# A decoder trunk on one core: the cross-attention's cached keys, cached values and memory projections in another order

## The reference

```python
def cross_attend(h, mk, mv, w_q, w_o):
    B, T, D = h.shape
    q = (h @ w_q).reshape(B, T, XATTN_HEADS, XATTN_HEAD_DIM)
    s = jnp.einsum('bthd,bmhd->bhtm', q, mk).astype(F32) * (XATTN_HEAD_DIM ** -0.5)
    p = jax.nn.softmax(s, axis=-1).astype(mv.dtype)
    o = jnp.einsum('bhtm,bmhd->bthd', p, mv).reshape(B, T, D)
    return o @ w_o
```

## Time and profile before

| | |
|---|---|
| median of 3 runs | 1862.55 us (1862.42 to 1863.79) |
| the profiled execution | 1862.46 us, span 1860.7 us |
| mean granted TensorE clock | 0.924 of full |
| busy: TensorE, DVE, ACT, GpSimd | 88%, 54%, 38%, 17% |
| cross-attention, from the norm's reciprocal to the output projection's start | 557.7 to 676.1 us (layer 0), 1476.3 to 1594.6 us (layer 1) |

### The profile page before, as it was taken

One profiled execution on the slowest core, in us unless ns is written; L12 is line 12 of the kernel. 1 busy time (PEld: TensorE's weight loads), 2 busy tenths in 40 slices (PEclk: granted clock), 3 DMA queues, 4 the chain that ended last, 5 costly groups with the idle time before them and its releaser, 6 DMA issues.

```text
span 1860.7 us, 32204 instructions
## 1 busy us (share of the span) xinstructions
PE 1645.3 (88%) x13842; PEld 1546.5 (83%) x13842; DVE 1008.2 (54%) x1467; ACT 711.2 (38%) x1206; POOL 319.2 (17%) x365
## 2 busy tenths in 40 slices
PE   7999989884779988999989998999755999799997
PEld 6999979772578868999989998988634997699996
DVE  5554467854455336554365544786564533465543
ACT  4443345221344324443344433452123443344432
POOL 0000006994010000000000001089920100100000
PEclk9999999886789989999989999998767999799999
DMA  5766634101534774445345575330034357634450
GB/s 223 264 246 256 245 117 139 39 2 37 182 145 141 298 285 136 159 165 175 136 158 204 207 297 202 136 114 20 2 115 159 114 212 281 254 136 159 161 175 30
DMA packets 39246, 303.66 MB, mean 163 GB/s; under 512 B 4736, under 2 KB 4896, under 8 KB 6304
## 3 DMA queue, kind: packets, MB, share of 16 engines
q1 hardware_dynamic: 36624, 287.67, 42.6%
q0 software_dynamic: 2192, 12.35, 2.2%
q10 hardware_dynamic: 288, 1.57, 0.2%
HBM read 291.82 MB, written 36.83 MB: 177 GB/s over the span
## 4 chain that ended last, share of the span: by engine, by line
PE 66%; POOL 15%; DVE 9%; ACT 4%; DMA 3%; issue 1%; SPq 0%; POOLq 0%; DVEq 0%; ACTq 0%
PE bank L565 21%; PE bank L566 20%; PE bank L567 20%; POOL arena L462 10%; POOL arena L478 4%; DMA slots<-stream 3%; ACT w_hi L1202 2%; DVE w_lo L1590 1%; DVE h_mem L1605 1%; DVE h_lo L1590 1%; DVE rs L1600 1%; PE bank L576 1%; PE bank L1118 1%; PE bank L1154 1%; PE bank L1103 1%
## 5 line engine op out<-in xcount | busy, mean ns | idle before, releaser
L1590 DVE TENSOR_TENSOR w_lo<-slots,w_hi 128x1024 fp32r<-128x1024 f32 x392 | 481.6, 1231 | 452.8 <-ACT w_hi L1202 452.3
L565 PE MATMUL bank<-h_hi,w_hi 128*128 128x288 f32 x2048 | 619.1, 302 | 39.3 <-DVE h_lo L1590 30.5
L566 PE MATMUL bank<-h_lo,w_hi 128*128 128x288 f32 x2048 | 611.2, 298 | 0.0
L567 PE MATMUL bank<-h_hi,w_lo 128*128 128x288 f32 x2048 | 609.1, 297 | 0.0
L1202 ACT CAST w_hi<-slots 128x1024 fp32r<-128x1024 f32 x392 | 410.1, 1048 | 392.0 <-PE bank L567 344.9
L565 PEld LDWEIGHTS bank<-h_hi,w_hi 128*128 128x128 f32 x2048 | 389.7, 190 | 48.3 <-DVE h_lo L1590 36.5
L567 PEld LDWEIGHTS bank<-h_hi,w_lo 128*128 128x128 f32 x2048 | 392.5, 192 | 0.0
L566 PEld LDWEIGHTS bank<-h_lo,w_hi 128*128 128x128 f32 x2048 | 391.8, 191 | 0.2
L566 PE MATMUL bank<-hid_lo,w_hi 128*128 128x288 f32 x704 | 208.2, 296 | 0.0
L565 PE MATMUL bank<-hid_hi,w_hi 128*128 128x288 f32 x704 | 208.1, 296 | 0.0
L567 PE MATMUL bank<-hid_hi,w_lo 128*128 128x288 f32 x704 | 206.8, 294 | 0.0
(11 more groups left out here) (281 smaller groups left out, 1939.7 us busy)
## 6 DMA issues: line engine op xcount, KB each, us to landing
slots<-stream SPq DMA_DIRECT2D x244, 1024.0 KB, 5.0
out_win3k<-win3k SPq DMA_DIRECT2D x2, 4080.0 KB
out_win3v<-win3v SPq DMA_DIRECT2D x2, 4080.0 KB
out_win2k<-win2k SPq DMA_DIRECT2D x2, 2032.0 KB
out_win2v<-win2v SPq DMA_DIRECT2D x2, 2032.0 KB
con<-consts SPq DMA_DIRECT2D x1, 2276.0 KB, 11.9
arena<-mem_in POOLq DMA_DIRECT2D x2, 1024.0 KB, 5.5
out_memk<-arena POOLq DMA_DIRECT2D x2, 1024.0 KB, 7.4
```

The source lines that it names most:

```text
L565: mm(out, lhs[0], rhs[0], start=start, stop=False)
L566: mm(out, lhs[0], rhs[1], start=False, stop=False)
L567: return mm(out, lhs[1], rhs[0], start=False, stop=stop)
L1590: D(tt(out, src, hi.bitcast(F32), ALU.subtract), name)
```

## The change

The slab order from kv 2 on becomes: kv 2, memk 0, kv 3, memk 1, memk 2, memk 3, kv 4, memk 4, memk 5, kv 5, memk 6, memk 7, kv 6, memv 0, memv 1, kv 7, memv 2 to 7, then o 0 to 3 as before (slabs 63 to 88). TensorE's order follows: after the prompt's scores come the samples' scores in pairs with the value blocks between them, then the samples' transposed probabilities and products with cached values two by two around value block 3, and the last four among the prompt's heads. On ACT the samples' exponentials and the copies of their transposed probabilities move ahead of value block 3's copies. On DVE row maxima come earlier, and the samples' `row_max(4)` and `weigh(4)` move in among the splits.

```diff
-for _i in range(MEMK_EARLY):
-    ORDER.remove(("memk", _i))
-    ORDER.insert(ORDER.index(("kv", _i + K_EARLY // 2)) + 1, ("memk", _i))
+_x = ORDER.index(("kv", K_EARLY // 2))
+_after_q = (("kv", (2,)), ("memk", (0,)), ("kv", (3,)), ("memk", (1, 2, 3)), ("kv", (4,)), ("memk", (4, 5)), ("kv", (5,)),
+            ("memk", (6, 7)), ("kv", (6,)), ("memv", (0, 1)), ("kv", (7,)), ("memv", range(2, 8)))
+ORDER[_x:ORDER.index(("o", 0))] = [(_name, _i) for _name, _some in _after_q for _i in _some]
```

TensorE, where `memory_values(n)` is the value block as before and `sample_values(b_)` one step of the former loop over the samples (for b_ = 0 with the wait for the samples' transposed probabilities in front):

```diff
+                memory_keys((4, 5))
+                sample_scores(0)
+                memory_keys((6, 7))
+                sample_scores(1)
+                prompt_scores()
+                sample_scores(2)
+                sample_scores(3)
+                memory_values(0)
+                sample_scores(4)
+                sample_scores(5)
+                memory_values(1)
+                sample_scores(6)
+                sample_scores(7)
+                memory_values(2)
+                probs_T(8)
+                sample_values(0)
+                sample_values(1)
+                memory_values(3)
+                sample_values(2)
+                sample_values(3)
+                for hd in range(4):
+                    probs_T(2 * hd)
+                    probs_T(2 * hd + 1)
+                    if hd:
+                        prompt_out(hd - 1)
+                    sample_values(4 + hd)
+                prompt_out(3)
```

ACT, where `memory_values(n)` copies the block's two banks and then splits `next_unit(kv_unit(KT + 2 * n + 1))`:

```diff
+                for n in range(4):
+                    xexp(2 * n)
+                    split(next_unit(kv_unit(KT + 2 * n)))
+                    xexp(2 * n + 1)
+                    if n == 2:
+                        xexp(6)
+                        xexp(7)
+                        xexp(8)
+                        memory_values(2)
+                        sample_probs_T()
+                        split(next_unit(kv_unit(KT + 6)))
+                        memory_values(3)
+                        break
+                    memory_values(n)
```

DVE:

```diff
                 for u in range(8):
-                    if u % 2 == 0 and u < 6:
-                        row_max(u // 2 + 1)
+                    if u < 3:
+                        row_max(u + 1)
+                    if u == 4:
+                        row_max(4)
                     split(next_unit(kv_unit(KT + u)))
+                    if u == 4:
+                        weigh(4)
                     if u % 2:
                         weigh(u // 2)
-                row_max(4)
-                weigh(4)
```

More of the change, by code:

```diff
@@ L49 @@
 NSLOT = 4
-MEMK_EARLY = 6
 K_EARLY = 4
@@ L1107, in sample_scores, with prompt_scores, memory_values @@
                         TL.done(i, ("xs", 8))
[L1109 to L1121, removed]
+                def prompt_scores():
+                    pe.wait_ge(scalar_done, SL.value(l, ("kx", KT - 1)))
+                    for u in range(8):
+                        hd, qt = divmod(u, 2)
+                        if qt == 0:
+                            claim(hd, (SL, ("xexp", u + 1)))
+                        for dt in range(2):
+                            i = mm(bank[hd][:, qt * MEM:(qt + 1) * MEM], qx[:, 2 * hd + dt, qt * P:(qt + 1) * P], kx[:, 2 * hd + dt, :],
+                                   start=dt == 0, stop=dt == 1)
+                        TL.done(i, ("xs", u))
+                def memory_values(n):
                     for mt in range(2):
@@ L1135, in _ @@
                                 TL.done(i, ("vx", n * 2 + mt))
-                    sample_scores(n + 2)
-                for b_ in range(MEMK_EARLY, DEC_BATCH):
-                    sample_scores(b_)
                 def probs_T(u):
@@ L1156, in prompt_out, with sample_values @@
                     TL.done(i, ("ox", hd))
[L1158 to L1168, removed]
+                def sample_values(b_):
+                    if b_ == 0:
+                        claim(5, (SL, "oxs"))
+                        pe.wait_ge(scalar_done, SL.value(l, ("xpT", 8)))
                     w = arrived(SLAB_AT["memv", b_]).rearrange("p (k c) -> p k c", k=2)
@@ L1175, in _ @@
                     TL.done(i, ("slab", SLAB_AT["memv", b_]))
-                TL.done(i, "oxs")
+                    if b_ == DEC_BATCH - 1:
+                        TL.done(i, "oxs")
+                memory_keys((4, 5))
[25 more added lines that the diff above has]
+                prompt_out(3)
                 claim(4, (VL, "oxs_lo"))
@@ L1520, in _ @@
                     split(next_unit(kv_unit(KT + 2 * n + 1)))
-                xexp(8)
                 def probs_T(u):
@@ L1544, in _ @@
                         prompt_out(hd - 1)
-                sample_probs_T()
                 prompt_out(3)
```

## The result

The changed kernel takes 1895.81 us (median of 4 runs, 1891.49 to 1896.62) against 1862.49 us: a ratio of 1.0176, 95% interval 1.0157 to 1.0195, so it is slower by 1.8%. The prediction had 1880.5 us and a range up to 1891. Its profiled execution took 1891.49 us with a span of 1889.7 us.

The account below looks back on a forecast made before the run. TensorE, 88% busy, was taken as the bound, except at cross-attention's end, where it waits for value slabs. Three new waits with clock loss gave +10.8 and +9.4 us by layer, less 2.2: +18.0, 1880.5 us, range 1865 to 1891.

Parts of the forecast that it names:

- The ring: Cross-attention transfers: four slots, SyncE issues slab n only when slab n-4 is released, so kv 4, 5 and 7 come later.
- Rival A: Cross-attention: kv slabs arrive in time and TensorE runs through, 13.0 us per layer saved, 1836.5 us; chance 0.08.
- First wait: Before the prompt's scores: TensorE idles for key copies behind kv 4's split, 4.7 us in layer 0, 3.3 in layer 1.
- The clock behind each wait: After each TensorE wait over 2.2 us: work at half clock loses 1.8 us, bounds 0 and 2.3.
- What comes back: At the output projection's start: the 2.3 us lost at half clock partly disappears, 1.1 us per layer taken.
- Landings: Slab transfers: one lands about 5.0 us after issue, each of several issued closely 2.46 us after the one before.
- Second and third wait: Before value block 1, 4.5 us behind kv 5's split; before the samples' transposes, 6.1 us behind kv 7's.
- The tail: End of cross-attention: four heads of 2.16 us with four slabs of 0.93, 12.3 us, then copies and projection start.
- The value slabs: Cached value transfers: six of eight no longer issued after the whole of the scores; the last ones not late.
- B: Cross-attention: waits come but the clock stays up or its loss falls into the next wait, 1869.7 us; chance 0.08.
- C: Cross-attention: gain and waits cancel, time within 0.2% of no change, which needs the third wait to vanish; chance 0.04.
- D: Cross-attention: stores and paired issues delay further landings, 2 us on each of two more per layer, 1889 us; chance 0.05.

Follow-up runs that it names:

- a1: Changed kernel with only the slab order altered, kv 4 to 7 each one pair earlier: 1848.92 us, ratio 0.9921 to the first kernel.
- d1: Changed kernel plus 7, 10 and 13 products of constants on TensorE in its three waits: 1879.46 us, ratio 1.0081 to the first kernel.
- b4: Changed kernel with a1's slab order and the samples' softmax, transposes and first two cached values behind value block 3: 1858.27 us, ratio 0.9961.
- a0: The changed kernel run again, unchanged, with a second profile: 1894.04 us, ratio 1.0164 to the first kernel.

## Why the prediction was wrong in size

**The ring, right.** "Kv 4 takes the second of the pair issued at 602.5 and 602.9": it was issued at 602.2 as the second of a pair and landed after 8.1 us. The three waits came at the three places, with the releasers named (ACT, ACT, DVE), and a1 removes them by list order alone. Rival A's mechanism exists, but only in a1's order: its condition, kv 4 split before about 606.5, is met there (the split starts at 602.23).

**First wait, right.** 4.7 and 3.3 us predicted, 4.24 and 3.16 measured in the first profile.

**The clock behind each wait, mis-sized: the largest of four terms that failed.** "I take 1.8 for each wait over 2.2 us", 10.8 for six. The runs show 14 to 15.5: d1 gives 15.5 at most, 14 if its shorter waits are taken off. The windows behind the six waits of the changed kernel, layer 0 and then layer 1, give the same:

```profile
613.00:619.00 6.00, 6.00 (x16) 4.79 (x17) 0.77 (x1) 0.00 (x0) 0.57 (x1) 0.55 0.43 176
638.00:643.00 5.00, 4.80 (x25) 4.83 (x26) 4.53 (x9) 1.61 (x4) 0.00 (x0) 0.58 0.54 180
661.00:667.00 6.00, 5.38 (x43) 2.99 (x44) 1.36 (x3) 0.43 (x2) 0.00 (x0) 0.57 0.30 81
1547.00:1554.00 7.00, 6.61 (x17) 5.31 (x18) 1.32 (x2) 0.34 (x2) 0.57 (x1) 0.53 0.57 235
1572.00:1578.00 6.00, 6.00 (x30) 6.00 (x31) 4.11 (x9) 2.04 (x4) 0.00 (x0) 0.54 0.72 261
1594.00:1598.00 4.00, 2.96 (x26) 1.61 (x30) 1.80 (x5) 0.43 (x2) 0.00 (x0) 0.50 0.00 0
```

Length times (1 - clock), less half of the idle time inside the window, is 2.7, 2.0, 2.3, 3.1, 2.8 and 1.5 us: 14.4 in all, 2.4 for a wait where 1.8 was taken. The 1.8 came from the earlier trace rows, where the low stretch lasted 3.4 us. The bound of 2.3 was the other row at hand, the projection's, and three of the six reach or pass it. Two rows gave no upper bound.

**What comes back, wrong.** I took 1.1 us per layer for the projection at full clock. In the changed kernel its start again ran at half for 5.5 us in layer 0 and 3.4 in layer 1 (0.72 from 1624 to 1630), against 4.6 and 4.4 before. In sum nothing came back: 2.2 us.

```profile
691.00:697.00 6.00, 5.64 (x24) 5.67 (x25) 2.48 (x3) 0.78 (x1) 0.00 (x0) 0.51 0.58 205
```

**Landings, short by over 1 us each.** Kv 5 was to land 6.6 us after issue and took 7.8; kv 7 6.6 and took 7.8. I had applied the even spacing of the earlier trace rows to slabs issued in close succession. Second and third wait: 4.5 and 6.1 us predicted, 6.12 and 7.45 measured in layer 0 (4.92 and 6.47 in layer 1). All six waits together: 29.2 us predicted, 32.4 measured. The fit of the Trainium skill (DMA: Bandwidth & Descriptors, "Anatomy of one DMA") for transfers issued by GpSimd would have gone the other way: by it an estimate of 4.4 us for a slab, where the first of the pair behind memk 0 landed in 4.9 to 5.0.

**The tail, short by about 1.8 us per layer.** From the end of the two cached values behind block 3 to the projection the walk had 686.9 - 670.8 = 16.1 us; it took 691.36 - 673.46 = 17.9 in layer 0 and 1624.00 - 1606.17 = 17.8 in layer 1. Of this 0.72 us is a wait for a slab, where "the last value slabs are not late here", and most of the rest is a pitch of 3.3 us for a head with its slab, where 2.16 + 0.93 was taken.

**The value slabs, a wrong reading without weight in the sum.** "Six of the eight are no longer issued after the whole of the scores": memv 2 to 7 still are. SyncE issued them at 648.6 and from 664.2 to 673.6 us; before the change memv 0 to 3 went out from 637.4 to 645.9 and memv 4 to 7 from 657.2 to 659.8. The products are spread, the transfers are later.

The sum, for the profiled execution: 29.1 - 18.0 = 11.1 us too little. The clock gives 3.6 (14.4 - 10.8), the waits 3.2, the tail 3.5, the projection 2.2, 12.5 together. Against them stand the value blocks, taken at 5.9 us where one at full clock lasts 5.6 (from 624.50 to 630.14): six to eight of them make 1.6 to 2.1 us. So the mechanism was right and no single size was far off; four terms erred the same way. On top the timed runs lie some 4 us above the profiled one, which the walk has no term for. The ends of the forecast's own range were not worked out well either: with its own terms they come to 1867.3 and about 1887 us, where it said 1866 and 1890.

**Rivals.** B (the clock stays up, or its loss falls into the next wait) is excluded by d1 and the windows above. C needs the third wait to vanish, and all three came. The cause of D, later landings, was present, but smaller than its 2 us for each of two more: the second and third wait were 1.6 and 1.4 us over the forecast in layer 0, 0.4 and 0.4 in layer 1. The order inside the engines is no cost once the slabs are in time (a1, b4).

## What to carry to other kernels

When transfers are reordered through a ring with few slots, follow each slab to the engine that reads it first, here ACT and DVE with their splits three units ahead, and ask what stands behind that read in the same engine's program; a slab that TensorE needs "later" may be needed by them now. The Trainium skill (Perfetto Trace Analysis, "Optimization Strategy") says that interleaving regimes may improve performance; a1 shows the gain, 0.8%, and the changed kernel shows that the same interleaving loses 1.8% with the weights one pair too late. Price an idle of TensorE as its length plus the half-clock stretch behind it: here waits of 3 to 7 us cost another 2.4 us on average, between 1.5 and 3.1.

## What the runs showed of the hardware

- The half-clock stretch after an idle is not of one length, and a longer idle does not make it longer. After 2.25 us idle it lasted 3.4 us and began 1.5 us behind the resumption. In the changed kernel, counted from the end of the idle, it lasted about 6.2, 5.5, 5.5, 3.9, 3.5 and 5.1 us behind idles of 3.16, 4.24, 4.92, 6.12, 6.47 and 7.45 us (windows above).
- The same two idles before the projection, 1.04 and 2.13 us with two transposes between, dropped the clock in both layers of the changed kernel (0.51 in 691 to 697). In a1 they left it full in layer 0 (the first two rows) and dropped it in layer 1 (the third), within one execution. So the length of these idles alone does not decide it:

```profile
666.00:669.00 3.00, 0.57 (x3) 0.39 (x4) 2.47 (x4) 3.00 (x5) 0.00 (x0) 1.00 0.98 407
669.00:675.00 6.00, 6.00 (x47) 6.00 (x47) 3.22 (x4) 1.65 (x3) 0.00 (x0) 1.00 0.57 191
1580.00:1586.00 6.00, 6.00 (x28) 6.00 (x28) 1.99 (x3) 0.00 (x0) 0.00 (x0) 0.53 0.57 197
```

- Of the two 1 MB loads issued 0.4 us apart when memk 0's slot comes free, the first lands after 4.9 to 5.0 us. The second landed after 7.0 us in layer 1 of the first profiles of both kernels, and after 8.0 to 8.4 in layer 0 of these and in both layers of a0. What decides it stays open.
